# Sums of squares and probability scaling on ScalarE, products with v in even steps: a hybrid layer kernel on Trainium2

## What is computed

```python
q_b = (rmsnorm(cq, mla_q_norm) @ w_uq).reshape(B, S, MLA_HEADS, hq)          # hq = 128 + 64
kv = (rmsnorm(ckv, mla_kv_norm) @ w_ukv).reshape(B, S, MLA_HEADS, 128 + 128)
k_nope, v_b = kv[..., :128], kv[..., 128:]
k_b = jnp.concatenate([k_nope, k_rope], axis=-1)
q_b = rmsnorm(q_b, q_head_norm)       # per token and head: needs the sum of squares of its 192 columns
k_b = rmsnorm(k_b, k_head_norm)
q_b, k_b = (first 128 columns as they are, last 64 rotated by position)
s = einsum('bhqd,bhkd->bhqk', q, k) * scale
p = softmax(s)
o = einsum('bhqk,bhkd->bhqd', p, v)
```

## Time and profile before

| | us |
|---|---|
| median of 3 runs (2098.37 to 2102.87) | 2099.53 |
| the profiled execution, its own time | 2103.23 |
| its span, first to last instruction | 2101.5 |
| PE busy / VectorE busy / ScalarE busy over the span | 1963.7 / 1297.3 / 966.9 |
| attention loop, first scores to last product | 149.4 to about 600 |
| mean granted TensorE clock | 0.967 of full speed |

### The profile page before, as it was taken

The page is one execution under the profiler, slowest core; times in us unless marked ns, Lnnn a source line. Parts: engine busy times, 40 slices in busy tenths (PEclk is TensorE's granted clock), DMA queues, the critical chain, the costliest instruction groups (busy, mean ns, idle before and its releaser), DMA issues.

```text
span 2101.5 us, 25676 instructions
## 1 busy us (share of the span) xinstructions
PE 1963.7 (93%) x9232; PEld 1624.5 (77%) x9232; DVE 1297.3 (62%) x1664; ACT 966.9 (46%) x1312; POOL 114.4 (5%) x125
## 2 busy tenths in 40 slices
PE   7988999999889999999999999998189999999997
PEld 5667888888768787877788778888168888888886
DVE  4157877777865646555311222433769898988986
ACT  3145555555454334243311211221158778787875
POOL 2000000000000000000000000000000101010100
PEclk9989999999999999999999999996589999999999
DMA  6000000000211111021412311343679999999993
GB/s 231 0 16 11 16 22 21 21 19 8 97 59 42 51 41 51 30 61 38 133 51 61 100 51 50 121 157 133 255 261 383 393 401 393 401 392 401 392 400 82
DMA packets 140445, 307.12 MB, mean 146 GB/s; under 512 B 16208, under 2 KB 70608, under 8 KB 140368
## 3 DMA queue, kind: packets, MB, share of 16 engines
q1 hardware_dynamic: 135760, 289.27, 37.1%
q0 software_dynamic: 4608, 16.78, 3.1%
HBM read 276.64 MB, written 29.36 MB: 146 GB/s over the span
## 4 chain that ended last, share of the span: by engine, by line
PE 85%; DVE 10%; DMA 2%; ACT 1%; issue 1%; POOL 0%; SPq 0%; DVEq 0%; ACTq 0%
PE ps L788 21%; PE ps L790 21%; PE ps L789 21%; PE ps L750 6%; PE ps L812 4%; PE ps L773 2%; PE ps L774 2%; DVE row_max L1359 1%; PE ps L1099 1%; PE ps L1000 1%; PE ps L1012 1%; PE ps L846 1%; PE ps L845 1%; DVE pT_lo L1189 1%; PE ps L896 1%
## 5 line engine op out<-in xcount | busy, mean ns | idle before, releaser
L1189 DVE TENSOR_TENSOR w_lo<-w_raw,w_hi 128x1024 fp32r<-128x1024 f32 x384 | 442.8, 1219 | 57.7 <-ACT w_hi L2014 57.5
L2014 ACT ACTIVATE w_hi<-w_raw 128x1024 fp32r<-128x1024 f32 x384 | 371.0, 1052 | 7.3 <-DMA w_raw<-in_w_gate_e 5.4
L1189 DVE TENSOR_TENSOR d_lo<-d_raw,d_hi 128x1024 fp32r<-128x1024 f32 x72 | 88.1, 1224 | 349.2 <-ACT d_hi L1841 349.1
L1841 ACT ACTIVATE d_hi<-d_raw 128x1024 fp32r<-128x1024 f32 x72 | 76.2, 1060 | 365.8 <-PE ps L790 349.2
L788 PE MATMUL ps<-w_hi,xeT_hi 128*128 128x512 f32 x512 | 202.4, 395 | 4.4 <-DVE w_lo L1189 2.9
L790 PE MATMUL ps<-w_hi,xeT_lo 128*128 128x512 f32 x512 | 201.0, 393 | 0.0
L789 PE MATMUL ps<-w_lo,xeT_hi 128*128 128x512 f32 x512 | 200.9, 392 | 0.0
L788 PE MATMUL ps<-hT_hi,d_hi 128*128 128x512 f32 x384 | 151.7, 395 | 4.4 <-DVE hT_lo L1189 2.6
L788 PE MATMUL ps<-d_hi,hT_hi 128*128 128x512 f32 x384 | 149.7, 390 | 1.3 <-DVE oaS L1435 1.3
L790 PE MATMUL ps<-hT_hi,d_lo 128*128 128x512 f32 x384 | 149.8, 390 | 0.0
L789 PE MATMUL ps<-hT_lo,d_hi 128*128 128x512 f32 x384 | 149.7, 390 | 0.0
(11 more groups left out here) (289 smaller groups left out, 3886.1 us busy)
## 6 DMA issues: line engine op xcount, KB each, us to landing
w_raw<-in_w_gate_e SPq DMA_DIRECT2D x128, 512.0 KB, 6.8
w_raw<-in_w_up_e SPq DMA_DIRECT2D x128, 512.0 KB, 6.8
w_raw<-in_w_down_e SPq DMA_DIRECT2D x128, 512.0 KB, 5.6
d_raw<-in_w_in SPq DMA_DIRECT2D x80, 256.0 KB, 3.1
d_raw<-in_w_o SPq DMA_DIRECT2D x32, 256.0 KB, 2.8
xs<-in_x SPq DMA_DIRECT2D x8, 512.0 KB, 7.2
rows_T<-hT SPq DMA_DIRECT2D x1, 4096.0 KB, 12.3
mla_out_T<-obS SPq DMA_DIRECT2D x16, 256.0 KB, 2.0
```

What stands on the lines that cost most here:

```text
L1189: return dve.tensor_tensor(dst, whole, high.bitcast(F32), ALU.subtract)
L1841: nc.scalar.activation(d_hi[:, n % 2, :], d_raw[:, n % 2, :], ACT.Copy).then_inc(d_hi_ok, 1)
L2014: nc.scalar.activation(w_hi[:, n % RING, :], w_raw[:, n % RAW, :], ACT.Copy).then_inc(hi_ok, 1)
```

## The change

The sums of squares are made by ScalarE as it takes each projection: after the copy, two more activations (one for each block) square the columns from PSUM and add them up by the engine's accumulator straight into `stat`. `head_sq` counts these, and takes the place of `prj_ev`, so bank 7 is given back after the second square, not after the copy. `q_squares`, `k_squares` and the two reductions are gone; `r_tmp`, which lay over `sq_q`, has memory of its own. VectorE keeps the reciprocals of the row sums and hands them over with a new semaphore `inv_ok`; ScalarE multiplies the tile, after `exponentials` in the loop. `values` takes two key blocks at each of the eight steps; at steps 1 and 5, where a half starts, it stands behind the projection. On VectorE the first `head_out` moves from step 1 to step 0, the mean of q's squares ahead of `v_low`, and the multiply of q's rotated part by its gains from `q_rotate` (step 6) to `q_gain` (step 5).

```diff
-PV_STEP = {0: (-1, 0, (4, 5)), 1: (-1, 0, (6, 7)), 2: (-1, 1, (0, 1, 2)), 3: (-1, 1, (3, 4, 5)), 4: (-1, 1, (6, 7)),
-           6: (0, 0, (0, 1)), 7: (0, 0, (2, 3))}
+PV_STEP = {5: (0, 0, (0, 1)), 6: (0, 0, (2, 3)), 7: (0, 0, (4, 5)), 0: (-1, 0, (6, 7)),
+           1: (-1, 1, (0, 1)), 2: (-1, 1, (2, 3)), 3: (-1, 1, (4, 5)), 4: (-1, 1, (6, 7))}
+HALF_STARTS = (1, 5)
...
                 elif count > 2:
-                    pe.wait_ge(prj_ev, count - 2)
+                    pe.wait_ge(head_sq, 2 * count - 4)
...
                 if bank == 7:
-                    pe.wait_ge(prj_ev, min(seam_count(h, c) + 5, group_count(MH - 1, 3)))
+                    pe.wait_ge(head_sq, 2 * min(seam_count(h, c) + 5, group_count(MH - 1, 3)))
...
-                if pv_at(i, n):
+                if n not in HALF_STARTS and pv_at(i, n):
                     values(*pv_at(i, n))
                 if i < MH and group_at(i, n):
                     project(*group_at(i, n))
+                if n in HALF_STARTS and pv_at(i, n):
+                    values(*pv_at(i, n))
...
-            def q_stats(h):
-                dve.wait_ge(head_sq, 2 * h + 2)
-                s.link(dve.tensor_reduce(stat[:, 4, :], sq_q[:], AX, ALU.add))
+            def q_mean(h):
+                dve.wait_ge(head_sq, 16 * h + 16)
                 mean_eps(stat[:, 4, :], stat[:, 4, :], HQ).then_inc(head_ms, 1)
...
-            def normalise(t):
+            def reciprocals(t):
                 n = t % NT
                 dve.wait_ge(exp_ok, t + 1)
-                s.link(dve.reciprocal(row_inv[:, n:n + 1], row_sum[:, n:n + 1]))
-                dve.tensor_scalar(probs[:, t % 3, :], probs[:, t % 3, :], row_inv[:, n:n + 1], None,
-                                  ALU.mult).then_inc(p_ok, 1)
+                dve.reciprocal(row_inv[:, n:n + 1], row_sum[:, n:n + 1]).then_inc(inv_ok, 1)
...
-                nc.scalar.activation(dst, ps[:, group_bank(h, g), 0:2 * width].rearrange("p (a c) -> p a c", a=2),
-                                     ACT.Copy).then_inc(prj_ev, 1)
...
+                src = ps[:, group_bank(h, g), 0:2 * width].rearrange("p (a c) -> p a c", a=2)
+                nc.scalar.activation(dst, src, ACT.Copy)
+                stat_at, cols = (4, HQ) if g < 4 else (5, NOPE)
+                if g == 0 and h:
+                    act.wait_ge(head_n, 3 * h - 1)
+                if g == 4 and h:
+                    act.wait_ge(head_n, 3 * h - 2)
+                if group_count(h, g) > 1:
+                    act.wait_ge(head_sq, 2 * group_count(h, g) - 2)
+                for j in range(2):
+                    t = 2 * (g % 4) + j
+                    ins = nc.scalar.activation(squares[:, j, 0:cols], src[:, j, 0:cols], ACT.Square,
+                                               accum_out=stat[:, stat_at, t:t + 1])
+                    ins.then_inc(head_sq, 1)
...
+            def normalise(t):
+                act.wait_ge(inv_ok, t + 1)
+                nc.scalar.activation(probs[:, t % 3, :], probs[:, t % 3, :], ACT.Copy,
+                                     scale=row_inv[:, t % NT:t % NT + 1]).then_inc(p_ok, 1)
...
+                if tile_at(i, n + 1) is not None and n < 2 and i == MH:
+                    normalise(tile_at(i, n + 1))
                 if i < MH:
                     exponentials(i, n)
+                    if tile_at(i, n + 1) is not None:
+                        normalise(tile_at(i, n + 1))
```

More of the change, by code:

```diff
@@ L252, in hybrid_layer @@
                         kRr = sb_in(head_mem, "kRr", [P, NT, 2 * ROPE])
-                        sq_q = sb_in(head_mem, "sq_q", [P, NT, HQ])
-                        r_tmp = sq_q[:, :, :].rearrange("p t c -> p (t c)")[:, 0:4 * NT * RH] \
-                            .rearrange("p (a t r) -> p a t r", a=4, t=NT)
+                        r_tmp = sb_in(head_mem, "r_tmp", [P, 4, NT, RH])
+                        squares = sb_in(head_mem, "squares", [P, 2, HQ])
                         qT_hi = sb_in(head_mem, "qT_hi", [P, S], F32R)
@@ L395, in hybrid_layer @@
         p_ok = sem("p_ok")
+        inv_ok = sem("inv_ok")
         p_tr = sem("p_tr")
@@ L1314, in q_gain, with q_rotate, k_mean @@
                                   ALU.mult).then_inc(head_n, 1)
-            def q_rotate(h):
                 dve.wait_ge(head_n, 3 * h + 2)
-                s.link(dve.tensor_tensor(qR[:, :, NOPE:HQ], qR[:, :, NOPE:HQ],
+                s.mark(dve.tensor_tensor(qR[:, :, NOPE:HQ], qR[:, :, NOPE:HQ],
                                          qhr_b[:].unsqueeze(1).broadcast_to((P, NT, ROPE)), ALU.mult))
+                return s.n
+            def q_rotate(gained):
+                s.wait(gained)
                 rotate(qR[:, :, NOPE:HQ + ROPE], qR[:, :, NOPE:HQ], r_tmp, s).then_inc(head_n, 1)
-            def k_stats(h):
-                dve.wait_ge(head_sq, 2 * h + 1)
-                s.link(dve.tensor_reduce(stat[:, 5, :], sq_q[:, :, 0:NOPE], AX, ALU.add))
+            def k_mean(h):
+                dve.wait_ge(head_sq, 16 * h + 8)
                 s.link(dve.tensor_tensor(stat[:, 5, :], stat[:, 5, :], stat[:, 3, :], ALU.add))
@@ L1385, in _ @@
             dve.wait_ge(k_rot_ok, 1)
-            k_stats(0)
+            k_mean(0)
             v_low(0)
             k_norm(0)
-            q_stats(0)
+            q_mean(0)
             for c in (4, 5):
                 seam_low(0, c)
-            q_gain(0)
+            gained = q_gain(0)
             for c in (6, 7):
                 seam_low(0, c)
-            q_rotate(0)
+            q_rotate(gained)
             for c in (0, 2):
@@ L1406, in _ @@
                 if tile_at(i, n + 1) is not None:
-                    normalise(tile_at(i, n + 1))
+                    reciprocals(tile_at(i, n + 1))
                 if n == 0 and i + 1 < MH:
-                    k_stats(i + 1)
+                    k_mean(i + 1)
+                if n == 0 and i:
+                    head_out(i - 1, 0)
                 if n == 1 and i + 1 < MH:
                     k_norm(i + 1)
-                if n == 1 and i:
-                    head_out(i - 1, 0)
                 if n == 4 and i:
@@ L1416, in _ @@
                 if n == 4 and i + 1 < MH:
+                    q_mean(i + 1)
                     v_low(i + 1)
-                    q_stats(i + 1)
                 if n == 5 and i + 1 < MH:
-                    q_gain(i + 1)
+                    gained = q_gain(i + 1)
                 if n == 6 and i + 1 < MH:
-                    q_rotate(i + 1)
+                    q_rotate(gained)
                 if i == MH - 1 and n >= 6:
@@ L1803, in v_high @@
                     act.wait_ge(pv_mm, 2 * h - 2)
-                act.wait_ge(prj_ev, group_count(h, 7))
+                act.wait_ge(head_sq, 2 * group_count(h, 7))
                 nc.scalar.activation(v_hi[h % 2], kvR[:, :, NOPE:NOPE + MV], ACT.Copy).then_inc(v_hi_ok, 1)
@@ L1868, in _ @@
                     take(*group_at(i, n))
-                if n == 3 and i + 1 < MH:
-                    q_squares(i + 1)
-                if n == 7 and i + 2 < MH:
-                    k_squares(i + 2)
                 if i == MH - 1 and n >= 6:
```

13 lines of the change are left out of this document (removed).

## The result

The changed kernel takes **2106.59 us** (median of 7 runs, 2105.39 to 2107.91) against 2099.53 for the kernel before (7 runs, 2097.78 to 2102.87). The ratio is **1.0034**, 95% interval 1.0024 to 1.0045: slower by a third of a per cent, 7.1 us. The prediction said 2105, with 2098 to 2112 as its range.

What follows compares the result with a forecast made beforehand. PE's own work was taken as the bound, VectorE and ScalarE costing only through PE's waits. Terms -2.4+1.4+2.1-1.7+5.9 = +5.3 on the profiled 2103.23 give 2108.5; the median lies 3.7 lower, so 2105 us, range 2098 to 2112.

Steps and rivals of the forecast that it cites:

- iteration 0: First attention iteration: step 5's wait arises, step 7's goes, six products (1.45 us) move up from the end: +1.4 us.
- iteration 6: Iteration without projection from step 4: q's gain ends earlier, PE waits 3.5 us for pT_lo: -1.7 us, clock left open.
- the end: Iteration 7 and drain: three pT_lo waits of 1.8 to 2.2 us, last two scalings' waits 1.5 and 1.3 longer: +5.9.
- Prices: ScalarE's instruction costs: a scaling 1.15-1.17 us, squares of 128 and 192 columns 0.31 and 0.36 us each.
- The rule on multiplications: Skill's advice to multiply on VectorE speaks against the change; at VectorE's price the sum would be some 3.5 us smaller.
- Step 4 to 5: Steady iteration: scaling ahead of v_hi delays copy and squares; new 1.25 us wait before seam transposes, step 5 0.55 longer.
- Step 1 and step 7: Steady iteration: projection at step 1 waits 0.85 us for the seam's low part; step 7's rotation wait goes, 1.0 gained.
- Rival (4): TensorE's clock falls in attention's last products: 2107.5 us; shares the forecast's chance of 0.54.
- (1): Rival, faster: the new wait at step 5 does not arise, an iteration -0.85 us, sum -5: 2094 us; chance 0.09.
- (2): Rival, no difference: scaling nearer VectorE's price, squares at 0.2, end 2 us shorter: +1, 2100.5 us; chance 0.24.
- (3): Rival, ScalarE too late: 0.6 us per square delays seam 7 in six iterations and the start: 2112 us; chance 0.13.
- (5): Rival: VectorE's load moves but nothing waited for it, iteration 6 gains nothing: +1.7, 2107 us; shares the forecast's 0.54.

Runs made afterwards that it cites:

- e6: Kernel before with only the scaling moved to ScalarE, squares and products as before: 2103.18 us, ratio 1.0017.
- e3: Changed kernel with the scaling back on VectorE, squares on ScalarE and even products kept: 2099.23 us, ratio 0.9999.
- e4: Changed kernel with the products with v as before and v_hi ahead of the scaling at step 4: 2086.97 us, ratio 0.9935.
- e5: Kernel before with only the squares moved to ScalarE and VectorE's new order for q: 2087.19 us, ratio 0.9958.
- e8: e4 with the last four tiles scaled by VectorE: 2083.18 us, ratio 0.9928.
- e1: Changed kernel with one line moved, so that ScalarE makes v_hi ahead of the scaling at step 4: 2097.58 us, ratio 0.9991.
- e9: Changed kernel with bank 7 given back at the copy and the squares read from SBUF after it: 2104.64 us, ratio 1.0025.
- e7: Kernel before with only the products spread evenly, two per step, behind the projection at steps 1 and 5: 2110.87 us, ratio 1.0066.
- e2: Changed kernel with the products with v placed as before, squares and scaling still on ScalarE: 2095.44 us, ratio 0.9975.

## Why the prediction was right, point by point

| term | predicted | measured, from the first projection |
|---|---|---|
| first scores | -2.4 | -2.1 |
| iteration 0 | +1.4 | +0.5 |
| iterations 1 to 5 | +2.1 | +2.8 |
| iteration 6 | -1.7 | -2.55 |
| the end | +5.9 | +5.7 |
| sum at the next stage's first product | +5.3 | +4.35 |
| the next stage | 0, clock up to +2.5 | +1.8 |

From the first projection to the end of the program the two profiles differ by 6.2 us, the medians by 7.1; the remaining 0.9 lies within the spread of the runs. The forecast of +5.3, on which 2105 rested, was 1.8 us low against the medians. That it is so near is partly luck: the attention part came out 1 us below the forecast, and the next stage, put at nothing, added 1.8. In the trace's own time the first scores start at 144.26 and the last product at 601.63, not at 147 and near 606, since this execution was 3 us ahead at the first projection.

**Prices.** The scaling takes 1.15 us (by form, count, busy us, mean ns, idle before; window of iteration 3), as estimated. The squares were costed too high:

```profile
L1845 ACT ACTIVATE probs<-probs,row_inv 128x1024 f32<-128x1024 f32 x8 | 9.2, 1150 | 0.6 <-DVE row_inv L1367 0.5
...
L1798 ACT ACTIVATE squares<-ps 128x192 f32<-128x192 f32 x8 | 2.5, 329 | 0.0
...
L1798 ACT ACTIVATE squares<-ps 128x128 f32<-128x128 f32 x8 | 2.1, 275 | 0.0
```

From start to start they take 0.25 us for 128 columns (355.65 to 355.90 above), where I took 0.31. ScalarE is busy 40.1 us per iteration, not 43; the prediction's own prices would have given about 41.6 (29.57 + 9.2 + 5.4, less 2.55 for the old squares).

**The rule on multiplications.** The Trainium skill ("ScalarE: Activation LUTs", "Rules for kernel authors") wants them on VectorE, and the prediction gave its price as some 3.5 us. This case bears the price out, 1.15 against 0.754 us. No run gives ScalarE VectorE's price, so the 3.5 us are not shown; taking the scaling off ScalarE altogether is worth 3.5 us by e6's median and 7.4 by e3's. But the rule goes by what one instruction costs. With `v_hi` ahead of it and the products as before, a scaling on ScalarE gives a steady iteration of 55.73 us (e4), and one on VectorE 56.36 (e5). The rule would cost 0.6 us per iteration there; with the scaling on VectorE step 5 is 0.37 us longer, in which the squares are waited for, and step 7 is 0.25 longer. At the end, where ScalarE's scaling is what PE waits for, the rule holds: e8 against e4 gains 4.6 us by the end's stretch, and 3.8 by the medians, whose intervals overlap.

**Step 4 to 5.** Predicted was a new wait of 1.25 us from start to start for the squares, then a projection 0.55 later. From the seam transposes of step 4 to the projection of step 5 it takes 10.01 us, 9.45 before: 0.56 longer, through the chain named: `v_hi`, `v_lo`, copy, squares. The profile puts the wait at 1.07. With the scaling behind `v_hi` (e1) none of it is left, and with the bank given back at the copy (e9) 0.50: the whole of it takes both, a late copy and squares that hold the bank behind it.

**Step 1 and step 7.** The new wait at step 1 costs 0.97 us from the seam to what follows the transposes (1.23 before, to the products; 2.20 now, to the projection), predicted 0.85; it was 0.73 by the profile, not the 0.5 to 0.6 that the last part of the prediction named. Step 7's is gone, as predicted. The sum per iteration is +0.57, not +0.4, within the 0.3 us I gave it.

**Iteration 0** is the largest miss within attention, +0.5 for +1.4, and it lies in step 0, which took 8.17 us here and 8.97 before. The rest of the iteration comes to +1.3. (The prediction's own values for its three parts, 0.55, -1.0 and 1.45, make +1.0; where its other 0.4 came from it doesn't say.) PE's work in step 0 is the same in both kernels. What differs is TensorE's clock: before, it was at half until the scores and the seam of that step were through, and here it was back at full with the seam, 4 us after the first scores. A window before and one after, each counted in its own trace:

```profile
154.00:155.00 1.00, 0.85 (x4) 0.45 (x3) 0.97 (x1) 0.12 (x1) 0.00 (x0) 0.50 0.00 0
```

```profile
148.50:149.00 0.50, 0.35 (x4) 0.10 (x1) 0.50 (x1) 0.12 (x1) 0.00 (x0) 1.00 0.00 0
```

The ten scores took 4.43 us before and 3.99 here, and from the seam to the projection it was 2.62 and 2.26. The prediction left this clock as it was.

**Iteration 6.** I predicted a 3.5 us wait for `pT_lo`, and named the clock as an unknown of -1.6. PE's timeline, steps 5 and 7:

```profile
531.80 0.50 PE L788 MATMUL ps<-pT_hi,v_hi_even 128*128 128x512 f32 x1 [3.16 <-DVE pT_lo L1191]
...
541.80 0.63 PE L750 MATMUL ps<-ident,qR 128*128 128x128 f32 x4 [0.98 <-DVE qR L1289]
```

A window behind the longer wait, the PE clock third from last:

```profile
532.00:535.00 3.00, 3.00 (x14) 2.42 (x14) 2.17 (x2) 1.01 (x1) 0.00 (x0) 1.00 0.00 0
```

The wait was 3.16 and the clock stayed at 1.00, 2.4 GHz, where the 4.46 us wait had left it at 0.50. So part of the unknown came true and the term went from -1.7 to -2.55. That was luck of this execution: in e9 the same wait is 3.17 long and the clock behind it is 0.50 (shown there), and iteration 6 takes 55.31 us, 1.05 less than before. In e7, where VectorE keeps its work, the same wait was 4.15 and the clock behind it 0.50:

```profile
536.00:539.00 3.00, 2.86 (x7) 2.29 (x8) 2.58 (x4) 0.00 (x0) 0.00 (x0) 0.50 0.00 0
```

The relief of VectorE that shortens this wait is mostly the squares'. PE in e3, which has the squares on ScalarE and the scaling on VectorE:

```profile
526.99 0.79 PE L788 MATMUL ps<-pT_hi,v_hi_even 128*128 128x512 f32 x1 [2.38 <-DVE pT_lo L1191]
```

From e7 to e3 the wait goes from 4.15 to 2.38; with the scaling on ScalarE it is 3.16 again, and 1.99 once `v_hi` stands ahead of the scaling (e1). In both e3 and e1 the clock is at 0.50 behind it.

**The end.** Three waits for `pT_lo` of 2.05, 1.64 and 1.57 (predicted 1.8 to 2.2 each, 1.7 by the profile), two for the scaling of 2.76 and 0.82 (2.2 or more each). The second is short because TensorE fell to half speed between them: the eight transposes at 588.97 took 1.97 us, those at 593.63 took 1.10, and part of the wait passed in them. In e9, where the clock was up at that place, the same two waits are 2.75 and 2.17. Two windows:

```profile
589.00:592.00 3.00, 3.00 (x12) 2.77 (x13) 2.10 (x3) 2.06 (x3) 0.00 (x0) 0.52 0.00 0
...
604.57:614.57 10.00, 10.00 (x37) 8.10 (x38) 8.19 (x7) 5.23 (x6) 4.35 (x6) 0.83 0.34 105
```

The second row is the beginning of the next stage, at 0.83 where the kernel before had 1.00:

```profile
603.21:613.21 10.00, 10.00 (x44) 8.31 (x45) 8.19 (x7) 5.24 (x6) 4.35 (x6) 1.00 0.33 104
```

It got through 37 matmuls in 10 us, the kernel before through 44. I put the 1.8 us of the last term down to it; no run takes it away by itself. All profiles but those of the kernel before and of e5 have such a fall at this place, e8's too, which has none in the drain. And what follows that first product, though it is the same work in every kernel, takes from 1494.5 us (e1) to 1500.7 (e2) in the eleven profiles, so 1.8 us of difference there need no cause in the change at all. Rival (4), the clock, thus came true in part, a little later than the last products.

**The rivals.** (1), faster, fell on the wait at step 5, which did arise: e1 removes it and is 9 us faster. With the products put back too (e4) the first rival's own time, 2094, is beaten by 7 us: a steady iteration gains 1.6 us there, where the rival had 0.85. (2), no difference to speak of, fell too: the interval begins at 1.0024, 5 us; the squares were nearly as cheap as it supposed, but the scaling cost 1.15 us and the end was no shorter than forecast by more than 0.2. (3), ScalarE too late, fell on the squares' price. (5), in which iteration 6 gains nothing, fell too: it gained 2.55 us.
